# The order of the retention's normalization and of the weight splits, and of the small loads' waits, in a two-block transformer kernel

## The chip, the core and the metric

The kernel runs as one program on one core of a Trainium2 chip. The metric is the device time of one execution in microseconds (us). Five engines work side by side, each through its own list of instructions in order, held back only by semaphores: TensorE (PE: matmuls, its weight loads shown as PEld), VectorE (DVE), ScalarE (ACT), GpSimd (POOL) and SyncE (SP), which issues most DMAs. ScalarE issues some small DMAs between its own instructions.

## The reference

Two transformer blocks one behind the other on x of 256 positions and 2048 features, float32. The part that matters here is the first block's token mixer, cut to what is computed:

```python
proj = h @ w_in                                   # q, k, v, g_ret, u, gate_r, gate_s
q, k = rope(q), rope(k) * 128 ** -0.5             # 8 heads, q and k 128 wide, v 256
scores = (q @ k^T) * decay                        # causal, one decay rate a head
ret = head_group_norm(scores @ v)                 # per position and head: mean, variance over 256
y_ret = (silu(g_ret) * ret) @ w_ret_out
y_ssm = gelu(s5_ssm(u))                           # 64 groups, 64 complex states each, a scan over positions
y_s5 = glu(y_ssm @ w_s5_glu)
merged = sigmoid(gate_r) * y_ret + sigmoid(gate_s) * y_s5
x = x + gt_m * rmsnorm(merged @ w_out) * gain     # then a SwiGLU block, then the second block
```

h is rmsnorm(x) scaled and shifted by a modulation that is itself a product of a vector c with the 2048 x 12288 matrix w_ada. A wide gated feed-forward follows, and a second block with another mixer and feed-forward.

## The kernel before

**Weights.** Every weight matrix comes in tiles of 1 MB (128 x 2048 words), through a ring of four slots. SyncE waits until TensorE is through with a slot (`slot_free`) and issues the next tile. ScalarE copies the tile to its rounded high part (`split_hi`, L1006, out ring_hi), VectorE subtracts that from the tile to get the low part (`split_lo`, L1490, out ring_lo). The low part overwrites the raw tile. TensorE then multiplies, in this stage with three matmuls a piece (L636 to L638). Step m of a stage splits the tile of step m + 2: that is `ahead(p, g, m)`, the same call on ScalarE and VectorE.

**Start (0 to about 150 us).** SyncE issues c, x, then in turns a pair of rows of w_ada (two slots of the ring) and a piece of the value weights. ScalarE issues the small loads (`start`): bias, gains, then six more counted by the semaphore `start_in`. ScalarE squares x tile by tile, TensorE adds the squares up with a matrix of ones (`add_squares(0)`, L685), ScalarE takes the root, VectorE multiplies each row pair by c (`row_pair`, L1512) and makes one scaled tile of h of it. TensorE multiplies the values of all heads as the tiles come (L730).

**Stage "heads".** Two heads an iteration g, four iterations, eight steps m of one weight tile each: q, k and the gate's two halves for either head. The first iteration is written out, the other three are a hardware loop. The products of head n come in steps with r = m mod 4. The work of the head before lies between them:

- r = 0: VectorE takes the turned output of head n - 1 times its gate (`ret_out`, L1723) and masks the scores of head n (`ret_masked`, L1750); TensorE multiplies these with the values (`ret_values`, L753 to L755) behind its product.
- r = 1: VectorE takes mean and variance of that product (`ret_stats`, L1734 to L1738); ScalarE takes the root (`ret_std`, L1167).
- r = 2: VectorE inverts it and makes the shift (`ret_scale`, L1743, L1744); ScalarE applies both (`ret_normed`, L1172) and prepares the decay of the next head (`ret_decay`, L1179, L1180); VectorE rotates q and k (`rotate`, L1763 to L1768), which empties the accumulator.
- r = 3: TensorE multiplies q and k (`ret_scores`, L748) and transposes the normalized output (`ret_back`, L761); ScalarE evacuates the gate (L1186).

**The state-space part** runs through the same steps of "heads" and the next stage, "ret". For each of 32 state tiles TensorE multiplies the input (L713); VectorE turns the result back and scans it (`s5_turned_back`, L1696 to L1703, at odd m); POOL turns it on (`turned_on`, L2215 to L2218) and scales the output matrix (`c_scaled`, L2225, L2227); TensorE multiplies these (L703). The sine and cosine tables of two state tiles are made by POOL's `angles` (L2199), ScalarE's `waves` (L1108 to L1110, at m = 6 and m = 1) and `cosines` (L1117, L1118), and POOL's `sines` (L2205). `s5_turned_back` at m = 1 waits for the tables that `sines(0)` finishes. At m = 2 VectorE and ScalarE alternate in a gelu (`s5_gelu`, L1711 to L1718).

**Stage "ret"** multiplies the merge gates and the retention's output weights, four iterations. Its first steps carry what is left of the last head; the last two pieces of its fifth product wait for that head's finished output (L1729). Nothing in the order is made by a scheduler: all of it is written out by hand.

## Time and profile before

| | |
|---|---|
| time, median of 3 runs | 3425.26 us (3423.00 to 3428.01) |
| the profiled execution's own time | 3423.0 us |
| its span | 3421.2 us |
| TensorE busy | 3321.9 us (97%) |
| VectorE busy | 2358.4 us (69%) |
| ScalarE busy | 1470.7 us (43%) |
| POOL busy | 421.8 us (12%) |
| DMA, mean over the span | 206 GB/s; 380 in the first fortieth |
| chain that ended last | TensorE 80%, VectorE 10%, issue 3%, ScalarE 2%, DMA 2% |

The busy shares are means over stages with different limits. "Idle before" in a timeline's row, in square brackets, is the time in which the engine stood still ahead of that instruction, with the one that released it. A row that merges several instructions runs from the first start to the last end.

### The profile page before, as it was taken

The numbers are of one execution on the slowest core, as the hardware profiler recorded it, in microseconds if no ns is written. First come the engines' busy times: TensorE is split into PE (matmuls) and PEld (weight loads), VectorE is DVE, ScalarE is ACT, GpSimd is POOL, SyncE is SP. The second block draws the span as 40 slices with busy tenths as digits, with TensorE's granted clock in tenths as the row PEclk, the third lists the DMA queues.
The fourth block names the chain that finished last, engine by engine and source line by source line (L and its number), as shares of the span: only waits on it lengthen the run. The fifth ranks groups of instructions, "written<-read, shape, count | busy, mean of one in ns | idle before, by whom it ended". The sixth has DMA issues, their size and how long they took to land.

```text
span 3421.2 us, 52033 instructions
## 1 busy us (share of the span) xinstructions
PE 3321.9 (97%) x20368; PEld 2944.1 (86%) x20368; DVE 2358.4 (69%) x2479; ACT 1470.7 (43%) x1504; POOL 421.8 (12%) x309
## 2 busy tenths in 40 slices
PE   7999999999989999999989999999999999999998
PEld 3598898899978888888868888888888888888887
DVE  6699889977676666656676567657677766666554
ACT  2256565444444444433354443443434444444332
POOL 1046567700200000000000000000002100000000
PEclk9999999999999999999999999999999999999999
DMA  9884445577735555567724444555555555554554
GB/s 380 346 315 164 166 179 208 223 295 301 270 135 185 194 185 192 188 244 264 261 99 168 164 161 181 188 184 190 185 194 191 185 192 188 187 193 182 192 190 147
DMA packets 126274, 706.34 MB, mean 206 GB/s; under 512 B 14160, under 2 KB 41424, under 8 KB 47840
## 3 DMA queue, kind: packets, MB, share of 16 engines
q1 hardware_dynamic: 115808, 695.96, 55.0%
q10 hardware_dynamic: 10368, 9.02, 0.8%
q8 instruction: 68, 1.11, 0.1%
q14 instruction: 30, 0.25, 0.0%
HBM read 702.83 MB, written 2.10 MB: 206 GB/s over the span
## 4 chain that ended last, share of the span: by engine, by line
PE 80%; DVE 10%; issue 3%; ACT 2%; DMA 2%; SPq 2%; POOL 1%; DVEq 0%; ACTq 0%; POOLq 0%
PE acc L639 44%; PE acc L640 24%; PE acc L636 3%; PE acc L638 3%; PE acc L637 3%; DVE ring_lo L1490 2%; SPq L543 1%; DVE ring_raw L1512 1%; DMA ring_raw<-w_ada 1%; ACT ring_hi L1006 1%; DVE s_w L1696 0%; PE p_norm L685 0%; DVE s_v L1697 0%; DMA ring_raw<-w_ret 0%; DVE aside_y L1512 0%
## 5 line engine op out<-in xcount | busy, mean ns | idle before, releaser
L1490 DVE TENSOR_TENSOR ring_lo<-ring_raw,ring_hi 128x2048 fp32r<-128x2048 f32 (+2 forms) x560 | 1277.2, 2282 | 564.2 <-ACT ring_hi L1006 563.0
L639 PE MATMUL acc<-h_split,ring_hi 128*128 128x512 f32 x4736 | 1655.7, 392 | 9.2 <-DVE h_split L1552 4.5
L640 PE MATMUL acc<-h_split,ring_lo 128*128 128x256 f32 x4736 | 1337.6, 282 | 0.0
L1006 ACT ACTIVATE ring_hi<-ring_raw 128x2048 fp32r<-128x2048 f32 (+2 forms) x560 | 1040.6, 1862 | 411.6 <-DMA ring_raw<-w_down 150.9
L639 PEld LDWEIGHTS acc<-h_split,ring_hi 128*128 128x128 f32 x4736 | 891.8, 188 | 197.3 <-issue 9.7
L640 PEld LDWEIGHTS acc<-h_split,ring_lo 128*128 128x128 f32 x4736 | 897.8, 190 | 0.4
L639 PE MATMUL acc<-ffn_split,ring_hi 128*128 128x512 f32 x1408 | 488.2, 390 | 0.0
L640 PE MATMUL acc<-ffn_split,ring_lo 128*128 128x256 f32 x1408 | 397.1, 282 | 0.0
L2157 POOL TENSOR_TENSOR sq_sum<-sq_sum,tile 128x256 f32<-128x256 f32 x60 | 77.1, 1286 | 2565.4 <-ACT tile L1032 2565.4
L636 PE MATMUL acc<-h_split,ring_hi 128*128 128x256 f32 x1152 | 328.1, 285 | 5.5 <-DVE ring_lo L1490 3.1
L637 PE MATMUL acc<-h_split,ring_hi 128*128 128x256 f32 x1152 | 321.6, 279 | 0.0
L638 PE MATMUL acc<-h_split,ring_lo 128*128 128x256 f32 x1152 | 321.4, 279 | 0.0
L639 PEld LDWEIGHTS acc<-ffn_split,ring_hi 128*128 128x128 f32 x1408 | 264.4, 188 | 55.4
L640 PEld LDWEIGHTS acc<-ffn_split,ring_lo 128*128 128x128 f32 x1408 | 266.1, 189 | 0.0
L636 PEld LDWEIGHTS acc<-h_split,ring_hi 128*128 128x128 f32 x1152 | 216.6, 188 | 7.6 <-issue 2.9
L637 PEld LDWEIGHTS acc<-h_split,ring_hi 128*128 128x128 f32 x1152 | 216.6, 188 | 0.9 <-issue 0.2
L638 PEld LDWEIGHTS acc<-h_split,ring_lo 128*128 128x128 f32 x1152 | 216.5, 188 | 0.0
L1323 ACT ACTIVATE ffn_split<-ffn_a 128x256 f32 (+1 forms) x88 | 36.9, 420 | 358.0 <-DVE ffn_a L1914 358.0
L1505 DVE TENSOR_REDUCE ffn_b<-acc 128x256 f32<-128x512 f32 x88 | 60.9, 692 | 140.3 <-PE acc L640 140.2
L1032 ACT ACTIVATE tile<-x_res 128x256 f32 (+1 forms) x80 | 33.2, 418 | 150.1 <-DVE x_res L2138 84.1
L1321 ACT ACTIVATE ffn_t<-ffn_a 128x256 f32<-128x256 f32 x88 | 36.9, 419 | 130.6 <-DVE ffn_a L1910 119.4
L1512 DVE CUSTOM_DVE_ANT_0 ring_raw<-ring_raw,c_act 128x2048 f32<-128x2048 f32 x32 | 72.8, 2294 | 28.3 <-DMA ring_raw<-w_ada 28.3
(384 smaller groups left out, 3994.9 us busy)
## 6 DMA issues: line engine op xcount, KB each, us to landing
ring_raw<-w_ff SPq DMA_DIRECT2D x88, 1024.0 KB, 4.8
ring_raw<-w_down SPq DMA_DIRECT2D x64, 1024.0 KB, 4.8
ring_raw<-w_ffb SPq DMA_DIRECT2D x56, 1024.0 KB, 4.8
ring_raw<-w_mix SPq DMA_DIRECT2D x48, 1024.0 KB, 4.8
ring_raw<-w_ada SPq DMA_DIRECT2D x32, 1024.0 KB, 11.0
ring_raw<-w_heads SPq DMA_DIRECT2D x32, 1024.0 KB, 4.9
ring_raw<-w_ret SPq DMA_DIRECT2D x32, 1024.0 KB, 5.3
ring_raw<-w_glu SPq DMA_DIRECT2D x32, 1024.0 KB, 4.8
```

What stands on the lines that cost most here:

```text
L636: mm(dst[:, 0:T], hi[s][:, t, :], moving[:, k, 0:T], start=start, stop=False)
L637: mm(dst[:, 0:T], hi[s][:, t, :], moving[:, k, T:], start=False, stop=False)
L638: return mm(dst[:, 0:T], lo[s][:, t, :], moving[:, k, 0:T], start=False, stop=stop)
L639: mm(dst[:], hi[s][:, t, :], moving[:, k, :], start=start, stop=False, skip_group_check=True)
L640: return mm(dst[:, T:], lo[s][:, t, :], moving[:, k, 0:T], start=False, stop=stop, skip_group_check=True)
L1006: run(hi[s][:, 0:n, :], raw[s][:, 0:n, :], COPY).then_inc(hi_done, 1)
L1321: run(t[i % 2][:], a[i % 2][:], ACT.Tanh, scale=0.5).then_inc(f_tanh, 1)
L1323: run(dst[:, 4 * g + (first + i), 0:T], a[i % 2][:], COPY, scale=0.5).then_inc(f_hi, 1)
L1490: tt(lo[s][:, 0:n, :], raw[s][:, 0:n, :], hi[s][:, 0:n, :], SUB).then_inc(lo_done, 1)
L1505: v.tensor_reduce(dst, acc[o % 2][:].rearrange("p (c t) -> p t c", c=2), AX_X, ADD).then_inc(sum_done, 1)
L1512: v.tensor_tensor_reduce(weights, weights, c_act[:], 1.0, 0.0, MUL, ADD, ada_sum[:, i:i + 1]).then_inc(done, 1)
L2157: tt(sq_sum[:], sq_sum[:], tile[b][:], ALU.add).then_inc(sq_used, 1)
```

## The change

No instruction is added or taken away. There are four parts.

**Waits for the small loads.** The load of `gains` moves into the group counted by `start_in`, behind s5_a, so the group has seven. TensorE waits for all seven ahead of the first sum of squares, VectorE ahead of the first row pair (where it waited for bias and gains), ScalarE where it waited for six. Ahead of the heads stage TensorE waits for ScalarE's first exponential (`s5_trig`), no more for the loads.

**ScalarE.** `ret_normed` is called ahead of `ahead` at r = 2, in "heads" and in the opening of "ret".

**VectorE.** At r = 1 `ret_stats` is called behind `ahead` and behind `s5_turned_back`; in the opening of "ret" behind `ahead`, and there ahead of `s5_turned_back`. At r = 2 `rotate` is called behind `ahead`.

**POOL.** The fourth `c_scaled` and `turned_on` of a group come ahead of `sines(0)` and `angles`.

```diff
@@ TensorE
             pe.wait_ge(ones_set, 2)
+            pe.wait_ge(start_in, 16 * 7)
             add_squares(0)
...
             pe.wait_ge(v_evac, 8)
-            pe.wait_ge(start_in, 16 * 6)
+            pe.wait_ge(s5_trig, 1)
@@ ScalarE, start()
                 act.dma_start(b_ada[:], dram["b_ada_c"]).then_inc(bias_in, 16)
-                act.dma_start(gains[:], dram["gains"]).then_inc(bias_in, 16)
-                for dst, name in ((s5_a, "s5_a"), (ident, "identity"), (rope, "rope"),
+                for dst, name in ((s5_a, "s5_a"), (gains, "gains"), (ident, "identity"), (rope, "rope"),
                                   (lag, "lag"), (log_g, "log_g"), (s5_d, "s5_d")):
@@ ScalarE, heads
+                    if r == 2 and some(n):
+                        ret_normed(n)
                     ahead(p, g, m)
                     s5_steps("heads", g, m, early=True)
...
                     elif r == 2:
-                        if some(n):
-                            ret_normed(n)
                         ret_decay(n)
@@ ScalarE, ret
+                    if opening(g) and m == 2:
+                        ret_normed(HEADS)
                     ahead(p, g, m)
...
-                        elif m == 2:
-                            ret_normed(HEADS)
@@ VectorE, start
-            dve.wait_ge(bias_in, 16 * 2)
+            dve.wait_ge(bias_in, 16)
+            dve.wait_ge(start_in, 16 * 7)
@@ VectorE, heads
-                    if r == 0 and some(n):
+                    if r == 2 and some(n):
+                        ret_scale(n)
+                    elif r == 0 and some(n):
                         if some(n - 1):
                             ret_out(n - 1)
                         ret_masked(n)
-                    elif r == 1 and some(n):
-                        ret_stats(n)
-                    elif r == 2:
-                        if some(n):
-                            ret_scale(n)
-                        rotate(p, g, m - 1, n)
                     ahead(p, g, m)
                     if r == 0 and some(n):
                         ret_gated(n)
                         if some(n - 1):
                             ret_done(n - 1, n - 2)
+                    elif r == 2:
+                        rotate(p, g, m - 1, n)
                     s5_turned_back("heads", g, m)
+                    if r == 1 and some(n):
+                        ret_stats(n)
                     s5_gelu("heads", g, m)
@@ VectorE, ret (opening only)
-                        elif m == 1:
-                            ret_stats(HEADS)
...
                     ahead(p, g, m)
                     if opening(g):
                         if m == 0:
                             ret_gated(HEADS)
                             ret_done(HEADS - 1, HEADS - 2)
+                        elif m == 1:
+                            ret_stats(HEADS)
@@ POOL, s5_group
                 turned_on(2, 4 * g + 2)
+                c_scaled(3, 4 * g + 3, 2 * g + 2)
+                turned_on(3, 4 * g + 3)
                 if not end:
                     sines(0, 2 * g + 2)
                     angles(2 * g + 3)
-                c_scaled(3, 4 * g + 3, 2 * g + 2)
-                turned_on(3, 4 * g + 3)
```

What stands in a row on ScalarE at m = 1 and m = 2 of the loop of "heads", before (ring_hi is the high part of a weight tile, o_t the normalized output, s_ph and s_sin the waves, ret_scale the semaphore of VectorE's L1744; ISA and REGISTER_ALU rows only set addresses and waits):

```order
L1167 ACTIVATE gn_mean<-gn_mean,eps 128x2 [waits ret_var]
L1107 REGISTER_ALU
L1108 ACT_TABLE_LOAD
L1108 ACTIVATE s_sin<-s_ph 128x512 [waits s5_angle]
L1109 ACTIVATE s_ph<-s_ph 128x512
L191 REGISTER_ALU
L1110 ACTIVATE s_ph<-s_ph,eps 128x512 [waits act_own]
L1005 ISA
L1006 ACTIVATE ring_hi<-ring_raw 128x2048 [waits raw_in0]
L1172 ACTIVATE o_t<-p_o,gn_shift,gn_mean 128x256 [waits ret_scale]
L1172 ACTIVATE o_t<-p_o,gn_shift,gn_mean 128x256
```

and with the change (line numbers from there on are one higher):

```order
L1167 ACTIVATE gn_mean<-gn_mean,eps 128x2 [waits ret_var]
L1107 REGISTER_ALU
L1108 ACT_TABLE_LOAD
L1108 ACTIVATE s_sin<-s_ph 128x512 [waits s5_angle]
L1109 ACTIVATE s_ph<-s_ph 128x512
L191 REGISTER_ALU
L1110 ACTIVATE s_ph<-s_ph,eps 128x512 [waits act_own]
L1172 ACTIVATE o_t<-p_o,gn_shift,gn_mean 128x256 [waits ret_scale]
L1172 ACTIVATE o_t<-p_o,gn_shift,gn_mean 128x256
L1006 ISA
L1007 ACTIVATE ring_hi<-ring_raw 128x2048 [waits raw_in0]
```

The high part's copy stood ahead of the normalization and now stands behind it; the root and the waves are where they were.

What stands in a row on VectorE at m = 5 and the beginning of its turn-back, before (ring_lo is the low part of a weight tile, s_w and s_v the state-space part):

```order
L1734 BN_STATS gn_stats<-p_o 128x6 [waits ret_summed,dve_own]
L1735 BN_STATS gn_stats<-p_o 128x6
L191 REGISTER_ALU
L1736 MEMSET gn_shift 128x2 [waits dve_own]
L1737 BN_AGGR gn_mean<-gn_stats 128x2
L1738 BN_AGGR gn_mean<-gn_stats 128x2
L1489 REGISTER_ALU
L1490 TENSOR_TENSOR ring_lo<-ring_raw,ring_hi 128x2048 [waits hi_done]
L1689 REGISTER_ALU
L1690 REGISTER_ALU [waits z_done]
L1696 TENSOR_TENSOR s_w<-p_z,s_tab 128x512 [waits scan_done,s5_sine,s5_cos]
L1697 TENSOR_TENSOR s_v<-p_z,s_tab 128x512
```

and with the change, from the same statistics on, into m = 6 (qk_rot is the rotation):

```order
L1735 BN_STATS gn_stats<-p_o 128x6 [waits ret_summed]
L1736 BN_STATS gn_stats<-p_o 128x6
L191 REGISTER_ALU
L1737 MEMSET gn_shift 128x2 [waits dve_own]
L1738 BN_AGGR gn_mean<-gn_stats 128x2
L1739 BN_AGGR gn_mean<-gn_stats 128x2
L1744 RECIPROCAL gn_mean<-gn_mean 128x2 [waits ret_std]
L191 REGISTER_ALU
L1745 SCALAR_TENSOR_TENSOR gn_shift<-gn_mean 128x2 [waits dve_own]
L1489 REGISTER_ALU
L1490 TENSOR_TENSOR ring_lo<-ring_raw,ring_hi 128x2048 [waits hi_done]
L1762 REGISTER_ALU [waits ret_done]
```

The statistics stood ahead of the low part's copy and of the whole turn-back, and now come directly ahead of the inverse and the shift; the next copy now stands ahead of the rotation.

What stands in a row on POOL at the end of its first group, before (s_tab is the sine table, s_ph the angles):

```order
L2218 TENSOR_TENSOR s_x<-s_x,s_w 128x256
L2205 TENSOR_TENSOR s_tab<-s_sin,s_ph 128x512 [waits s5_waves]
L2199 TENSOR_TENSOR s_ph<-s_turn 128x512 [waits s5_sine]
L2225 TENSOR_TENSOR s_prod<-s_c_sb,s_f 128x128 [waits s5_c_in1]
L2227 TENSOR_TENSOR s_c_sb<-s_prod 128x2x32 [waits pool_own]
L2215 TENSOR_TENSOR s_x<-s_w,s_tab 128x512 [waits y_part,s5_scanned]
L2216 TENSOR_TENSOR s_w<-s_w,s_tab 128x512
L2217 TENSOR_TENSOR s_x<-s_w,s_x 128x256 [waits pool_own]
L2218 TENSOR_TENSOR s_x<-s_x,s_w 128x256
```

and with the change:

```order
L2218 TENSOR_TENSOR s_x<-s_x,s_w 128x256
L2225 TENSOR_TENSOR s_prod<-s_c_sb,s_f 128x128 [waits s5_c_in1]
L2227 TENSOR_TENSOR s_c_sb<-s_prod 128x2x32 [waits pool_own]
L2215 TENSOR_TENSOR s_x<-s_w,s_tab 128x512 [waits y_part,s5_scanned]
L2216 TENSOR_TENSOR s_w<-s_w,s_tab 128x512
L2217 TENSOR_TENSOR s_x<-s_w,s_x 128x256 [waits pool_own]
L2218 TENSOR_TENSOR s_x<-s_x,s_w 128x256
L2205 TENSOR_TENSOR s_tab<-s_sin,s_ph 128x512 [waits s5_waves]
L2199 TENSOR_TENSOR s_ph<-s_turn 128x512 [waits s5_sine]
```

The sine table and the angles stood ahead of the fourth state tile's steps and now stand behind them.

## Rows read from the trace of the kernel before

**Rows 1.** windows: us, busy us (instructions) by engine, clock, DMA share, GB/s

```profile
205.00:455.00 250.00, 231.90 (x1779) 224.15 (x1778) 228.03 (x272) 150.24 (x170) 149.27 (x111) 0.99 0.50 183
```

**Rows 2.** waits of TensorE, 205 to 455: who, for whom, us, times, longest

```profile
PE p_o L753 <- DVE scores L1750: 16.0, 8, 3.6
```

**Rows 3.** timeline, VectorE, odd half: start, us, line, operation [idle before <-releaser]

```profile
302.81 0.43 DVE L1734 BATCH_NORM_STATS2 gn_stats<-p_o 128x6 f32<-128x256 f32 x1
...
303.78 2.26 DVE L1490 TENSOR_TENSOR ring_lo<-ring_raw,ring_hi 128x2048 fp32r<-128x2048 f32 x1
...
309.53 1.27 DVE L1744 SCALAR_TENSOR_TENSOR gn_shift<-gn_mean 128x2 f32<-128x2 f32 x1
...
312.84 1.25 DVE L1768 TENSOR_TENSOR qk_rot<-qk_rot,qk_sin 128x512 f32<-128x512 f32 x1
...
319.05 3.02 DVE L1490 TENSOR_TENSOR ring_lo<-ring_raw,ring_hi 128x2048 fp32r<-128x2048 f32 x1 [2.75 <-ACT ring_hi L1006]
...
325.97 0.55 DVE L1750 SCALAR_TENSOR_TENSOR scores<-p_score,scores 128x384 f32<-128x384 f32 x1
```

**Rows 4.** timeline, ScalarE, odd half

```profile
303.89 0.30 ACT L1167 ACTIVATE gn_mean<-gn_mean,eps 128x2 f32<-128x2 f32 x1 [5.22 <-DVE gn_mean L1738]
304.10 1.90 ACT L1006 ACTIVATE ring_hi<-ring_raw 128x2048 fp32r<-128x2048 f32 x1
310.84 1.02 ACT L1172 ACTIVATE o_t<-p_o,gn_shift,gn_mean 128x256 f32<-128x256 f32 x2 [4.84 <-DVE gn_shift L1744]
311.88 1.28 ACT L1179 ACT_TABLE_LOAD   x1
...
314.00 1.28 ACT L1108 ACT_TABLE_LOAD   x1
...
317.11 1.91 ACT L1006 ACTIVATE ring_hi<-ring_raw 128x2048 fp32r<-128x2048 f32 x1
```

**Rows 5.** timeline, VectorE, even half

```profile
330.57 1.23 DVE L1729 SCALAR_TENSOR_TENSOR ret_split<-qk_sin,ret_split 128x512 f32 x1
...
340.65 0.94 DVE L1768 TENSOR_TENSOR qk_rot<-qk_rot,qk_sin 128x512 f32<-128x512 f32 x1
...
350.38 2.29 DVE L1490 TENSOR_TENSOR ring_lo<-ring_raw,ring_hi 128x2048 fp32r<-128x2048 f32 x1 [1.23 <-ACT ring_hi L1006]
...
356.80 0.55 DVE L1750 SCALAR_TENSOR_TENSOR scores<-p_score,scores 128x384 f32<-128x384 f32 x1
```

**Rows 6.** timelines of VectorE and POOL: a copy, and POOL's work beside such

```profile
225.19 2.82 DVE L1490 TENSOR_TENSOR ring_lo<-ring_raw,ring_hi 128x2048 fp32r<-128x2048 f32 x1
...
225.81 3.36 POOL L2205 TENSOR_TENSOR s_tab<-s_sin,s_ph 128x512 f32<-128x512 f32 x1
...
331.21 1.19 POOL L2218 TENSOR_TENSOR s_x<-s_x,s_w 128x256 f32<-128x256 f32 x1
```

**Rows 7.** timelines of ScalarE and VectorE, opening of the ret stage

```profile
458.42 0.30 ACT L1167 ACTIVATE gn_mean<-gn_mean,eps 128x2 f32<-128x2 f32 x1 [0.85 <-DVE gn_mean L1738]
...
466.44 0.99 ACT L1172 ACTIVATE o_t<-p_o,gn_shift,gn_mean 128x256 f32<-128x256 f32 x2
...
479.11 0.69 DVE L1729 SCALAR_TENSOR_TENSOR ret_split<-qk_sin,ret_split 128x512 fp32r<-128x512 f32 x1 [0.70 <-ACT ret_split L1163]
...
518.09 0.69 DVE L1696 TENSOR_TENSOR s_w<-p_z,s_tab 128x512 f32<-128x512 f32 x1 [0.64 <-POOL s_x L2218]
```

**Rows 8.** the start: a DMA issue (xcount, KB, us to landing), then timelines

```profile
s_d_sb<-s_d ACTq DMA_DIRECT2D x1, 4.0 KB, 14.7
...
4.74 0.52 ACTq L1080 DMA_DIRECT2D s_d_sb<-s_d  x1
...
11.02 10.81 PE L685 MATMUL p_norm<-tile,ones 128*128 128x256 f32 x32 [11.02 <-ACT tile L1032]
...
28.38 3.96 SPq L527 DMA_DIRECT2D ring_raw<-w_ada  x4
...
38.17 2.29 DVE L1512 CUSTOM_DVE_ANT_0 ring_raw<-ring_raw,c_act 128x2048 f32<-128x2048 f32 x1 [5.20 <-DMA ring_raw<-w_ada]
```

More of the change, by code:

```diff
@@ L1066, in s5_waves_begin @@
             def s5_waves_begin():
-                act.wait_ge(start_in, 16 * 6)
+                act.wait_ge(start_in, 16 * 7)
                 run(s5_t[:, 0, :], s5_a[:, 2, :], ACT.Exp).then_inc(s5_trig, 1)
@@ L1809, in _ @@
                 for m in range(8):
-                    if opening(g):
-                        if m == 0:
-                            ret_out(HEADS - 1)
-                            ret_masked(HEADS)
-                        elif m == 1:
-                            ret_stats(HEADS)
-                        elif m == 2:
-                            ret_scale(HEADS)
+                    if opening(g) and m == 2:
+                        ret_scale(HEADS)
+                    elif opening(g) and m == 0:
+                        ret_out(HEADS - 1)
+                        ret_masked(HEADS)
                     ahead(p, g, m)
```

## The prediction

> **What bounds the kernel now.** I read first the windows of the whole span by engine, then who waits for whom, then the timeline of each engine through one iteration of the stage where TensorE waits. In the heads stage (about 205 to 455 us) TensorE is busy 231.90 of 250 us, VectorE 228.03 [rows 1]: two engines are near their limit at once, so what is put late on VectorE has little room. The wait list of TensorE there has one large entry: eight waits of 16.0 us together for the masked scores of L1750 [rows 2]. So the stage runs at the pace of the chain that ends in L1750, and nothing behind it has room either (TensorE is busy 97% of the whole span, in the small table above); a microsecond added to that chain is a microsecond of the kernel.
>
> One iteration of the stage is two heads. I call the steps from one L1750 to the next the odd half (m = 4 to 7, then L1750 at m = 0) and the even half (m = 0 to 3, then L1750 at m = 4). The timelines show both: L1750 ends at 326.52 and at 357.35 [rows 3, 5]. What the reader is to see in them: VectorE idles before its weight copies for ScalarE (2.75 us before the copy at 319.05 in the odd half, 1.23 us before that at 350.38 in the even half), and ScalarE in turn idles for VectorE (5.22 us before the square root, 4.84 us before `ret_normed`, L1172) [rows 3 to 5]. ScalarE gets its weight split (L1006, 304.10) done inside that second idle time. The two engines hand work back and forth, and each hand-over's place in the order is the whole question.
>
> **The change in the heads stage.** It adds no instruction. Statistics (L1734 and on) come behind the low-part copy and the turn-back of the state-space part; `ret_normed` comes ahead of ScalarE's weight split; on VectorE the rotation comes behind the copy that waits for that split. Read together: the split of tile m + 2 now stands behind `ret_normed`, which stands behind `ret_scale`, which stands behind the statistics. What was a free filler has become a link in the chain.
>
> Odd half, from 302.81, where the statistics began [rows 3, 4]. Copy 2.26 -> 305.07. Turn-back with the reciprocal: from the end of the copy (306.04) to the start of L1744 (309.53) 3.49 -> 308.56. Statistics 302.81 to 303.78, 0.97 -> 309.53. Square root 0.30 -> 309.83. L1744 took 1.27 beside POOL; I take that -> 311.10. `ret_normed` 1.02 -> 312.1. Weight split 1.90 -> 314.0, against 306.00 before. VectorE waits for it, then copies 2.26 -> 316.3, then rotates (310.80 to 314.09, 3.29) -> 319.6, against 314.09. ScalarE goes on with the decay (311.88 to 314.00, 2.12) -> 316.1, the waves (to 317.11, 3.11) -> 319.2, the next split 1.91 -> 321.1, against 319.02. VectorE's copy 2.26 -> 323.4, and from there to the end of L1750 it is 4.45 (322.07 to 326.52) -> 327.9. That is 1.4 us late. The rise is small because the 2.75 us of idle time takes most of it in. Bounds: 0.1 if L1744 (two values per row) costs next to nothing once POOL lets go of it, 2.2 if the last copy keeps its 3.02. In the first iteration VectorE also multiplies modulation rows at every second step, and has no such idle time to give: 1.4 + 2.75 = 4.1 (the lower bound stays 0.1). Four odd halves: 4.1 + 3 x 1.4 = 8.3.
>
> Even half, from 331.80, the end of L1729 [rows 5]. Copy 2.26, turn-back 3.49, statistics 0.97, square root 0.30 -> 338.8. Here ScalarE has the waves next (m = 1), which used to run while VectorE turned back: 3.11 -> 341.9. Only then `ret_normed` 1.02 -> 342.9 and the split 1.90 -> 344.8. VectorE, ready since about 339, waits; copy 2.26 -> 347.1; rotation 3.29 -> 350.4, against 341.59. From the rotation's end to the next copy it was 8.79 (341.59 to 350.38), of which the copy now done was 2.82, as long as that at 225.19 [rows 6]: 5.97 -> 356.4. From there to the end of L1750 it is 6.97 -> 363.3, against 357.35: 6.0 late. Nothing gives this back, since TensorE is the one that waits at the end of it. Bounds 5.4 (part of the two short waits on ScalarE inside the gelu chain goes) and 6.6 (the copy takes 2.8). Three even halves: 18.0.
>
> ScalarE's switches of function table are in these sums at their measured length: the load at 311.88 takes 1.28 and the function follows at once [rows 4]. The Trainium skill (ScalarE: Activation LUTs, What ACT_TABLE_LOAD costs) gives 2.66 us for each switch, 1.38 of it a drain. By that rule the wave step alone would make each even half 1.4 dearer, 4 us in all; the row shows no drain, so the row stands.
>
> **The opening of the next stage.** The last head is handled the same way at m = 1 and 2 of the ret stage. Its square root was at 458.42 and its `ret_normed` at 466.44 [rows 7]. The root moves behind a copy and the turn-back (2.26 + 3.3), to 464.0. Then 0.30, a table load 1.28, a gate's evacuation (short like the root, taken at 0.4), the waves 3.11 -> 469.1, so `ret_normed` is 2.7 late, and the split and the copy behind it (0.99 + 1.90 + 2.26) end at 474.3, some 5.4 late. The last two tiles of the fifth product wait for this head's finished output (L1729, 479.11, and it idled 0.70 there [rows 7]). I take 4.7, one short wait being given back; bounds 2.7 and 5.4.
>
> **The change on POOL.** The fourth `turned_on` now comes ahead of `sines(0)` and `angles`. Before, these filled a wait. Now `sines(0)` starts when L2218 ends (331.21 + 1.19 = 332.40) [rows 6], just when VectorE's moved copy is running, and the turn-back at m = 1 waits for it. The nearest row is L2205 at 225.81: started 0.62 behind a copy of VectorE (225.19) it took 3.36 [rows 6]. So 332.4 + 3.4 = 335.8, against 334.1 when VectorE arrives: 1.7. If nothing held it, it would take some 1.3 as its companions do, 333.7, and cost nothing; so 0 to 1.7, and I take 1.7, by that row. It stands before every even half and the ret opening: 4 x 1.7 = 6.8. In the ret stage the turn-back at 518.09 already waits for L2218 [rows 7], so one L2205 of 1.3 comes on top once: 8.1 in all, bounds 0 and 8.1.
>
> The Trainium skill (SBUF — State Buffer, Who interferes with whom) says that a VectorE instruction with two SBUF inputs and a GpSimd instruction that reads SBUF exclude each other for the whole instruction, whoever came first. By that rule `sines(0)` behind the copy costs what I took; the trace agrees at 225.81, where L2205 ends 1.16 behind the end of the copy (228.01).
>
> **The change at the start.** TensorE's sum of squares and VectorE's first row pair now wait for seven small loads. The last, s_d_sb, is issued at 4.7 and lands 14.7 later, 19.4 [rows 8]. TensorE began at 11.02 and took 10.81 [rows 8], so the norm comes 8.4 later. Behind it on TensorE stand the value products, on VectorE all row pairs. But the third pair's rows landed only at 38.17, after 5.20 us of idle time of VectorE [rows 8]: the transfers set the pace there, and its delay is taken in. The engines must not run dry meanwhile. Slots are freed at most 8.4 later, so their refills are issued at most 8.4 later, and rows issued at 28.38 land at 38.17 [rows 8], a backlog of 9.8. I cost it at nothing; if that cover is gone it is the full 8.4. Below nothing it can't go, since nothing is earlier. The new wait of the heads stage (for the exponential in place of the loads) is satisfied long before.
>
> **Sum.** 8.3 + 18.0 + 4.7 + 8.1 = 39.1. The profiled execution took 3423.0 (span 3421.2 and 1.8 around it), so 3462.1; the median of the three runs is 2.3 above the profiled one, so I state 3464. Its own range: low end 4 x 0.1 + 3 x 5.4 + 2.7 + 0 = 19.3, 3444; high end 4.1 + 3 x 2.2 + 3 x 6.6 + 5.4 + 8.1 = 44.0, 3469.
>
> **Rivals.** All are on the same base of 3425.
> - POOL's edit is free because `sines(0)` slips in between VectorE's instructions. Terms without 8.1: 31.0, 3456. For it: L2218 at 331.21, beside VectorE's work, took only 1.19 [rows 6]. Against: 225.81.
> - The even half costs no more than the odd one, as TensorE and VectorE regroup so that the waves lie under other work: 8.3 + 3 x 1.4 + 2.7 = 15.2, 3441. Against: ScalarE runs in order, and the waves stand between the root and `ret_normed`.
> - The start is not covered: a gap in the DMA stream is never made up, 8.4 more, 3472. For it: 8.4 is not far below the backlog of 9.8, and a gap is there for good once it is. Against: the 5.20 us of idle time, which shows that the data, not the slots, were late.
> - Faster: the point is the wait of TensorE for L1750. If ScalarE had the split done by the time VectorE asks for it, the earlier copy and earlier transposes would remove those waits, at most 16.0, 3409. It decides at one place: whether the split of tile m + 2 ends before `ret_scale` does. In the working above it ends 2.9 (314.0 against 311.1, odd) and some 5.8 (344.8 against about 339, even) behind.
> - The edits do nothing measurable: the reordered instructions have slack everywhere. The 16.0 us of waits speak against.
>
> **Numbers.** Forecast 0.65, free POOL edit 0.15, cheap even half 0.07, uncovered start 0.07, faster 0.04, nothing 0.02. A difference within 0.2% (7 us) is what a measurement of this kernel can't tell from none. Slower 0.94, same 0.02, faster 0.04. The range 3444 to 3476 takes in both ends of the sum and the start partly or wholly uncovered; it leaves out the cheap even half, the fast case and the null.
>
> **What would show it.** In the profile after: ScalarE's weight split behind `ret_normed` in both halves; VectorE idle some 3 and some 6 us for "ring_hi" before the copies of m = 6 and m = 2; TensorE's waits for the masked scores well above 16.0, and new ones of some 3 us for the rotated q and k ahead of the scores product; an even half, from one masked-scores instruction to the next, of some 38.5 us where it was 30.8 (326.52 to 357.35); the turn-back at m = 1 waiting for POOL; the sum of squares beginning at 19.4 and the third row pair still near 38. I am wrong if the even half stays near 31, or if the delay of the start is still there at 150 us.

## The result, and the profile after it

The changed kernel takes 3453.52 us, the median of four runs (3450.71 to 3458.48), against 3426.29 for the kernel before in the same series (3423.00 to 3428.01). The ratio is 1.0083, 95% interval 1.0064 to 1.0100: slower by some 28 us, within 22 to 34. The profiled execution took 3455.24, its span 3453.5.

The waits of TensorE in the heads stage, columns as in [rows 2]:

```profile
PE p_score L749 <- DVE qk_rot L1769: 16.8, 6, 3.6
PE p_o L754 <- DVE scores L1751: 16.0, 7, 4.8
```

The wait for the masked scores is no larger than in [rows 2]. A second one of the same size has come: for the rotated q and k. The stage as a whole, columns as in [rows 1], 276 us where there were 250:

```profile
206.00:482.00 276.00, 241.98 (x1781) 232.61 (x1780) 222.86 (x274) 150.04 (x170) 137.25 (x110) 0.95 0.46 164
```

VectorE is busy 222.86 us against 228.03 [rows 1]: it has not more to do, it stands still. (TensorE's 241.98 against 231.90 us are nearly the same instructions, 1781 and 1779, at a granted clock of 0.95 in place of 0.99; the last section says what that cost.) Where VectorE stands still, its timeline says. The odd half, against [rows 3]:

```profile
318.39 0.41 DVE L1735 BATCH_NORM_STATS2 gn_stats<-p_o 128x6 f32<-128x256 f32 x1
...
323.96 2.29 DVE L1490 TENSOR_TENSOR ring_lo<-ring_raw,ring_hi 128x2048 fp32r<-128x2048 f32 x1 [2.89 <-ACT ring_hi L1007]
...
331.10 2.29 DVE L1490 TENSOR_TENSOR ring_lo<-ring_raw,ring_hi 128x2048 fp32r<-128x2048 f32 x1 [2.11 <-ACT ring_hi L1007]
...
337.29 0.55 DVE L1751 SCALAR_TENSOR_TENSOR scores<-p_score,scores 128x384 f32<-128x384 f32 x1
```

The 2.75 us of [rows 3] have become 2.89 and 2.11. The half grows by only 1.5 us, because VectorE's instructions take 1.2 less in it (busy 27.46 us between 374.36 and 407.97, where it was 28.68 between 356.80 and 388.91): POOL runs beside fewer of them. The even half, against [rows 5] and [rows 6]:

```profile
343.05 2.82 DVE L1490 TENSOR_TENSOR ring_lo<-ring_raw,ring_hi 128x2048 fp32r<-128x2048 f32 x1
347.11 0.69 DVE L1697 TENSOR_TENSOR s_w<-p_z,s_tab 128x512 f32<-128x512 f32 x1 [1.24 <-POOL s_tab L2205]
...
358.21 2.29 DVE L1490 TENSOR_TENSOR ring_lo<-ring_raw,ring_hi 128x2048 fp32r<-128x2048 f32 x1 [4.54 <-ACT ring_hi L1007]
...
362.54 0.69 DVE L1769 TENSOR_TENSOR qk_rot<-qk_rot,qk_sin 128x512 f32<-128x512 f32 x1
...
364.11 0.29 DVE L1714 TENSOR_SCALAR s_g<-s_g 128x256 f32<-128x256 f32 x1 [0.48 <-ACT s_g L1148]
...
368.17 2.29 DVE L1490 TENSOR_TENSOR ring_lo<-ring_raw,ring_hi 128x2048 fp32r<-128x2048 f32 x1 [1.23 <-ACT ring_hi L1007]
...
374.36 0.55 DVE L1751 SCALAR_TENSOR_TENSOR scores<-p_score,scores 128x384 f32<-128x384 f32 x1
```

and ScalarE in it:

```profile
351.95 0.30 ACT L1167 ACTIVATE gn_mean<-gn_mean,eps 128x2 f32<-128x2 f32 x1 [9.71 <-DVE gn_mean L1739]
352.26 1.28 ACT L1108 ACT_TABLE_LOAD   x1
...
355.37 1.00 ACT L1172 ACTIVATE o_t<-p_o,gn_shift,gn_mean 128x256 f32<-128x256 f32 x2
356.27 1.91 ACT L1007 ACTIVATE ring_hi<-ring_raw 128x2048 fp32r<-128x2048 f32 x1
...
363.66 0.42 ACT L1148 ACTIVATE s_g<-s_y 128x256 f32<-128x256 f32 x1 [2.09 <-DVE s_y L1712]
```

The root of the same half in the kernel before:

```profile
332.80 0.30 ACT L1167 ACTIVATE gn_mean<-gn_mean,eps 128x2 f32<-128x2 f32 x1 [1.87 <-DVE gn_mean L1738]
```

From masked scores to masked scores it is 37.07 us (337.29 to 374.36) where it was 30.83 (325.97 to 356.80). Three pieces: up to ScalarE's root 14.66 (351.95) against 6.83 (332.80); from there to the copy that waits 1.23, 16.22 against 17.58 (350.38 in [rows 5]); and 6.19 against 6.42. The root is 7.8 us later, and 1.6 come back behind it. The root waits for the statistics, hence ScalarE's 9.71 us of idle time. VectorE's busy time in the half is the same as before (27.37 and 27.38 us): all of the 6.2 us is waiting.

The start of the program, against [rows 8]:

```profile
19.68 5.60 PE L685 MATMUL p_norm<-tile,ones 128*128 128x256 f32 x15 [19.68 <-DMA s_d_sb<-s_d]
```

```profile
38.55 2.29 DVE L1512 CUSTOM_DVE_ANT_0 ring_raw<-ring_raw,c_act 128x2048 f32<-128x2048 f32 x1
```

The sum of squares is 8.66 us late, the third row pair 0.38: the 5.20 us in which VectorE waited for the transfer [rows 8] are used up, and no more was needed. ScalarE's first weight split stands where it stood, at 147.06 (147.14 before), so nothing of the delay is left at 150 us.

### The profile page after: what moved, and what is told of

Its sections match the earlier page's. It is cut to its first block, busy times and chain, and to the rows that moved or that the text cites. A ratio compares the mean times of both kernels' runs of the same rounds, so it can differ in the third digit from the quotient of the medians.

```text
span 3453.5 us, 52031 instructions
## 1 busy us (share of the span) xinstructions
PE 3330.1 (96%) x20368; PEld 2951.9 (85%) x20368; DVE 2346.6 (68%) x2479; ACT 1468.3 (43%) x1504; POOL 412.9 (12%) x309
## 4 chain that ended last, share of the span: by engine, by line
PE 78%; DVE 8%; issue 4%; POOL 4%; ACT 3%; DMA 2%; SPq 1%; ACTq 0%; DVEq 0%; POOLq 0%
PE acc L639 44%; PE acc L640 23%; PE acc L636 3%; PE acc L637 3%; PE acc L638 3%; DVE ring_lo L1490 1%; ACT ring_hi L1007 1%; DVE ring_raw L1512 1%; POOL s_w L2216 1%; POOL s_x L2218 1%; PE p_norm L685 1%; POOL s_x L2215 1%; DMA ring_raw<-w_ada 1%; SPq L543 1%; POOL s_tab L2205 1%
## 5 line engine op out<-in xcount | busy, mean ns | idle before, releaser
L1490 DVE TENSOR_TENSOR ring_lo<-ring_raw,ring_hi 128x2048 fp32r<-128x2048 f32 (+2 forms) x560 | 1273.2, 2275 | 595.2 <-ACT ring_hi L1007 593.7
L637 PEld LDWEIGHTS acc<-h_split,ring_hi 128*128 128x128 f32 x1152 | 219.8, 191 | 0.9 <-issue 0.2
L639 PE MATMUL acc<-mixed_split,ring_hi 128*128 128x512 f32 x256 | 90.0, 394 | 0.0
```

The costliest lines, as they stand in the source:

```text
L637: mm(dst[:, 0:T], hi[s][:, t, :], moving[:, k, T:], start=False, stop=False)
L639: mm(dst[:], hi[s][:, t, :], moving[:, k, :], start=start, stop=False, skip_group_check=True)
L1490: tt(lo[s][:, 0:n, :], raw[s][:, 0:n, :], hi[s][:, 0:n, :], SUB).then_inc(lo_done, 1)
```

## The experiments

All were measured the same way. An iteration of the heads stage repeats to 0.1 or 0.2 us inside a run, so the table gives the distances between masked-scores instructions (us, read from each kernel's timeline of VectorE) beside the times. *Span of eight* is from the first to the eighth of them; where single ones differ (by 0.5 at most) the table gives their mean.

| kernel | first odd | odd | even | span of eight | median us | ratio (95%) |
|---|---|---|---|---|---|---|
| before | 30.9 | 32.1 | 30.7 | 219.3 | 3426.3 | |
| changed | 33.2 | 33.6 | 37.1 | 245.4 | 3453.5 | 1.0083 (1.0064-1.0100) |
| start_only | 30.9 | 32.1 | 30.7 | 219.2 | 3422.8 | 0.9996 (0.9986-1.0006) |
| act_only | 32.5 | 33.9 | 30.6 | 226.0 | 3430.7 | 1.0016 (1.0007-1.0026) |
| stats_only | 32.1 | 32.8 | 33.2 | 230.3 | 3435.9 | 1.0035 (1.0021-1.0049) |
| rotate_only | 30.9 | 32.1 | 30.8 | 219.5 | 3423.0 | 1.0000 (0.9990-1.0010) |
| pool_only | 30.2 | 31.5 | 31.7 | 219.8 | 3427.3 | 1.0004 (0.9995-1.0014) |
| after_no_pool | 34.2 | 34.3 | 35.6 | 244.1 | 3449.8 | 1.0072 (1.0055-1.0089) |
| after_no_rotate | 32.9 | 33.7 | 34.9 | 238.9 | 3447.8 | 1.0067 (1.0052-1.0083) |
| after_no_stats | 32.6 | 33.2 | 32.9 | 230.8 | 3440.5 | 1.0042 (1.0027-1.0058) |
| after_waves | 33.2 | 33.7 | 36.5 | 243.7 | 3451.8 | 1.0080 (1.0063-1.0096) |
| after_ret_waves | 33.2 | 33.7 | 37.1 | 245.6 | 3453.9 | 1.0093 (1.0076-1.0110) |
| masked_early | - | - | - | 216.6 | 3423.3 | 0.9995 (0.9986-1.0005) |
| masked_splits | - | - | - | 210.2 | 3415.0 | 0.9973 (0.9962-0.9985) |

The two last rows have their masked scores at m = 3 and 7, so their halves are others; an iteration is 62.8 and 60.1 us in them, 62.8 before, 70.7 with the change. The ratio of each experiment is to runs of the kernel before beside it (medians 3422.9 to 3425.4); the times of different rows are a little less comparable than the spans.

### The five parts, each alone

The diff of each is its part of the change as shown above. **start_only.** 

> The kernel before with the start's part of the change alone (gains counted with the small loads, all seven waited for ahead of the first sum of squares and the first row pair). Theory: the sum of squares begins near 19.5 in place of 11.0, and the transfers of the modulation's rows take the delay in; the first masked scores of the heads stage come at most 1.0 us later than the 232.25 of before, and the whole is within 2 us of before. Rival (a gap at the start is never made up): 8.4 us slower, first masked scores near 240.6.

The first masked scores are at 232.11, against 232.25. The start's part costs nothing. (In the changed kernel they are at 233.30, and about as late in act_only, 233.23, which leaves the start alone. Up to there the traces differ by 1 to 2 us whatever the edit; most of it comes at about 142 us, from TensorE's clock, as the last section shows.)

**act_only.** 

> The kernel before with ScalarE's part alone (the normalization ahead of the weight split). Theory (ScalarE is the pace-maker behind the normalization): decay, waves and the next split come one split (1.9 us) later, VectorE waits 4.65 in place of 2.75 before its copy in the odd half, and each of seven halves is 1.9 longer: 13 us slower. Rival (the edits cost only together, since the split is ahead of the statistics' chain as long as these are early): within 2 us of before.

Half right. In the odd half VectorE waits 4.53 as expected and the half is 1.8 longer. The even half is not longer at all: VectorE is the late one in the gelu there (in the kernel before ScalarE idles 1.71 us ahead of its L1148 at 344.75), so a split's delay on ScalarE is taken in (the 1.71 are 0.45 here, before L1148 at 349.49). 6.6 us in this stage, 7 in the median, where 13 were expected.

**stats_only.** 

> The kernel before with VectorE's late statistics alone (behind the copy and the turn-back). Theory: the split stands behind the root on ScalarE, so it is late even without the other edit; odd halves 0.9 longer, even halves 2.3 to 4.6 longer since the waves stand between the root and the split: 11 to 17 us slower, most of it in the even halves. Rival (the statistics have room, only the normalization ahead of the split makes the chain): within 2 us of before.

Odd 0.7 (first 1.2), even 2.5: the lower end of what was expected, 11.0 in this stage, 12 in the median. The rival is out. The theory holds for the odd half: VectorE waits 3.61 us for the split where it waited 2.75. In the even half the split is late, too (16.3 us behind the masked scores, 10.3 before), but the copy does not wait for it, as the rotation still stands ahead of it:

```profile
342.85 1.20 DVE L1744 SCALAR_TENSOR_TENSOR gn_shift<-gn_mean 128x2 f32<-128x2 f32 x1
...
347.67 3.14 DVE L1490 TENSOR_TENSOR ring_lo<-ring_raw,ring_hi 128x2048 fp32r<-128x2048 f32 x1
```

There 1.0 of the 2.4 us from 329.40 to 362.66 is waiting for ScalarE (0.36 for the root, 1.08 in place of 0.49 before the gelu's L1713), and 1.5 is VectorE's own instructions, which run beside other work of POOL (busy 28.85 us in place of 27.38; L1744 took 0.16 at 338.42 in the kernel before). The expectation had the right size there for the wrong reason.

**rotate_only.** 

> The kernel before with the rotation behind the low part's copy alone. Theory: VectorE does the same work in the other order, the scores product had stood in line behind TensorE's own product until 316.3 anyway; within 2 us of before. Rival (the scores product is what the masked scores wait for): 2.3 us later in each half, 16 us slower.

Free, as the theory had it: 0.2 us in the stage.

**pool_only.** 

> The kernel before with POOL's part alone (the fourth turn-on ahead of the sine table and the angles). Theory of the prediction: the turn-back at m = 1 waits for the sine table that runs beside the copy, 1.7 us before each even half, at most 8.1 in all. Reading of the changed kernel's trace: that wait is 1.24 there (347.11), so 1.2 in each of three even halves and 0.4 in the opening of ret, 3 to 5 us slower. Rival (the table slips in between): within 1 us.

In this stage only 0.5 us, but by two effects of opposite sign: even halves 1.0 longer, odd ones 0.6 shorter. Behind it, from the last masked scores to the weight split at 660 us, it is 3.6 more, so 4.1 in this trace. The medians show 2.0, and their interval (0.9995 to 1.0014) tells that neither from nothing nor from the 3 to 5 expected.

What the five add to the span of eight is -0.1, 6.6, 11.0, 0.2 and 0.5, 18.2 us in sum. Together they make 26.0. Nearly 8 us come only from the company. (All of these are for the heads stage alone.)

### One part taken back

**after_no_rotate.** 

> The changed kernel with the rotation back ahead of the low part's copy. Theory (the late split alone costs VectorE little as long as the rotation, 3.3 us of ready work, stands ahead of the copy that waits for it; behind the copy it holds the gelu up): the wait before the copy of m = 2 falls from 4.54 to about 1.3, the gelu begins 2 us sooner, ScalarE's 2.09 us of idle time before it go; the even half falls from 37.1 to 35.1, the odd half stays at 33.6 (there ScalarE's next split sets the time), 6 us faster than the changed kernel. Rival (the whole loss is in the statistics and ScalarE's order, the rotation is as free here as it was alone): both halves as in the changed kernel, within 2 us.

```diff
 VectorE, heads, r == 2
                         ret_scale(n)
+                    rotate(p, g, m - 1, n)      # and not behind ahead
```

As expected: 34.9 and 33.7, 5.7 us in the median. The same edit is worth 0.2 us alone and 6.5 in company (245.4 less 238.9). Its VectorE in the even half:

```profile
354.65 2.29 DVE L1490 TENSOR_TENSOR ring_lo<-ring_raw,ring_hi 128x2048 fp32r<-128x2048 f32 x1 [0.83 <-ACT ring_hi L1007]
...
358.35 0.30 DVE L1714 TENSOR_SCALAR s_g<-s_g 128x256 f32<-128x256 f32 x1 [1.02 <-ACT s_g L1148]
```

The copy waits 0.83 where it waited 4.54, since the rotation fills the time; and now the gelu waits for ScalarE and not the reverse.

**after_no_stats.** 

> The changed kernel with the statistics back ahead of the copy and the turn-back. Theory (ScalarE's root is the head of its chain to the split of m = 3, and it is 7.8 us late only because the statistics are): the root comes 6.8 us behind the masked scores again, the even half is 31.6 (30.8 and POOL's 1.0), the odd half 33.3 (the 1.8 of the normalization ahead of the split, less 0.6), some 16 us faster than the changed kernel, 3437. Rival (the normalization ahead of the split, with the rotation behind the copy, is the chain, and the statistics are only carried along): even half 35 or more, less than 6 us faster.

```diff
 VectorE, r == 1
+                        ret_stats(n)            # ahead of ahead, as before; the same in the opening of ret
```

The largest part: 14.6 us of the 26.0. The odd half is 33.2 as expected, the even one 32.9 and not 31.6. ScalarE and VectorE show why:

```profile
343.27 0.63 ACT L1108 ACTIVATE s_sin<-s_ph 128x512 f32<-128x512 f32 x1 [2.36 <-POOL s_ph L2199]
346.13 1.02 ACT L1172 ACTIVATE o_t<-p_o,gn_shift,gn_mean 128x256 f32<-128x256 f32 x2 [0.94 <-DVE gn_shift L1745]
...
348.98 2.51 DVE L1490 TENSOR_TENSOR ring_lo<-ring_raw,ring_hi 128x2048 fp32r<-128x2048 f32 x1 [2.89 <-ACT ring_hi L1007]
```

The root is back (6.8 us behind the masked scores), and the waves behind it wait 2.36 us for POOL's angles. That wait costs nothing here: it is over 0.94 us before the normalization gets VectorE's shift, and in pool_only it is as long (2.35). Up to the shift the two kernels run alike, 13.43 us from the masked scores. What is left is what the expectation forgot: with the normalization ahead of the split and the rotation behind the copy, VectorE has nothing to do until the split is there, 2.89 us. Of that, 1.7 come back, as its instructions down to the gelu take less time than in pool_only (the gelu's TENSOR_SCALAR 0.29 where it took 1.14), and the even half is 1.1 longer than pool_only's in all.

**after_no_pool.** 

> The changed kernel without POOL's part. Theory: the even half falls from 37.1 by the 1.24 us that the turn-back waited for POOL, to 35.9, and the whole is 3 to 5 us faster than the changed kernel. Rival (the wait is taken in by what comes behind it): even half still 37.1.

Even half 1.5 shorter, a little more than the 1.24; odd half 0.7 longer; 3.7 us in the median. Whence the odd half's part? VectorE's last copy of the odd half there:

```profile
330.67 3.02 DVE L1490 TENSOR_TENSOR ring_lo<-ring_raw,ring_hi 128x2048 fp32r<-128x2048 f32 x1 [2.12 <-ACT ring_hi L1007]
```

and POOL beside it:

```profile
330.48 1.06 POOL L2199 TENSOR_TENSOR s_ph<-s_turn 128x512 f32 x1 [0.28 <-POOL s_tab L2205]
```

It is the 3.02 of [rows 3]. With POOL's part the sine table and the angles have gone from here, and the copy takes 2.29 (331.10 above). They stand beside the even half's first copy in place of it:

```profile
343.68 3.34 POOL L2205 TENSOR_TENSOR s_tab<-s_sin,s_ph 128x512 f32<-128x512 f32 x1
```

3.34 where it takes 1.29 with nothing beside it (328.91 in after_no_pool), as [rows 6] had shown at 225.81. The collision was not made, it was moved, from a place where it cost 0.7 to one where it costs 1.5.

### Two tests of the mechanism

**after_waves.** 

> The changed kernel, but in the heads stage the waves of m = 1 stand behind the weight split of m = 2 on ScalarE, in place of ahead of the normalization. Theory (the waves between root and normalization are what makes the even half dear): normalization and split come 3.1 minus the 1.3 that the scaling takes anyway, some 1.9 us sooner; the even half falls from 37.1 towards 35.2, 5 to 6 us faster over three. Rival (the even half is dear because the gelu chain with its hand-overs follows behind, and the waves only change places): even half 37 or longer, since the waves now delay decay and cosines.

```diff
 ScalarE, heads: not at the end of m = 1 but
                     elif r == 2:
+                        if m == 2: waves(1, 2 * g + 1)
                         ret_decay(n)
```

0.6 to 0.7 us an even half, not 1.9: nearer to the rival. VectorE:

```profile
355.62 2.29 DVE L1492 TENSOR_TENSOR ring_lo<-ring_raw,ring_hi 128x2048 fp32r<-128x2048 f32 x1 [2.89 <-ACT ring_hi L1007]
...
362.54 0.29 DVE L1716 TENSOR_SCALAR s_g<-s_g 128x256 f32<-128x256 f32 x1 [1.45 <-ACT s_g L1148]
```

The split does come sooner (2.89 of wait in place of 4.54), but now the gelu waits 1.45 for ScalarE. From the late root to the end of the gelu ScalarE has the same work in any order. So the waves' place between root and normalization is not what makes the even half dear; that the root itself is late, and all of ScalarE's work stands behind it, is.

**after_ret_waves.** 

> The changed kernel, but in the ret stage ScalarE's waves of m = 1 stand behind the weight split of m = 2 (the heads stage is untouched). POOL's part of the change cost 2.8 us in this stage, where one of 1.3 was forecast. Theory (ScalarE's waves wait 3.62 us for POOL's angles, which now stand behind the fourth turn-on, and hold up the split and VectorE's copy behind them): the copy of m = 2 waits no more for the split (1.28 and 1.17 in the changed kernel), and up to 3 us of the ret stage are got back, 3451. Rival (it is VectorE's turn-back, which waits 2.03 us for the sine table itself, and moving ScalarE's waves changes nothing): within 1 us of the changed kernel at the end of the stage.

```diff
 ScalarE, ret: waves(1, ...) at m = 2 behind ahead, in place of m = 1
```

The copy's wait for the split is gone (1.28 before L1490 at 551.66), but the gelu behind it now waits 2.19 us for ScalarE where it waited 0.57, and the time is the same (3453.9). VectorE still has:

```profile
546.67 0.69 DVE L1700 TENSOR_TENSOR s_w<-p_z,s_tab 128x512 f32<-128x512 f32 x1 [2.04 <-POOL s_tab L2208]
```

The rival holds at this place. Compared split by split on ScalarE, after_no_pool is 26.9 us behind the kernel before at 489 us and 27.0 at 660, the changed kernel 28.2 and 31.1: POOL's part costs 2.8 us in between. This kernel, too, has 31.1 at 660. It entered the stage 1.3 us earlier (last masked scores at 477.41, not 478.67), lost that in the opening (the gelu waits 2.18), and is level with the changed kernel from there on. What makes up the 2.8 beside the wait of 2.04 was not taken apart.

### Is there more to gain?

**masked_early.** 

> The kernel before, with the masked scores (L1750) taken ahead of the copy at m = 3 and m = 7, one step earlier, where VectorE stood idle for ScalarE. Theory (the 16.0 us of TensorE's waits in the heads stage are VectorE's order, not its amount of work): these waits vanish, and 8 to 16 us of the kernel with them. Rival (VectorE is full, the wait moves to the copy that the next product needs): within 4 us of before.

```diff
 VectorE, heads
-                        ret_masked(n)           # r == 0
+                    elif r == 3:
+                        ret_masked(n + 1)       # ahead of ahead; the call in the opening of ret goes
```

The rival was right in size. The wait went over to TensorE's next product, not the one that the rival named: to L713, which waits until VectorE's turn-back has emptied p_z:

```profile
PE p_z L713 <- DVE s_v L1697: 12.6, 6, 2.9
```

The 16.0 us of [rows 2] were the place where TensorE met VectorE's pace, not a cost of that order.

**masked_splits.** 

> The kernel before with three moves in the heads stage: the masked scores ahead of the copy at m = 3 and 7; ScalarE's waves of m = 6 behind the split of m = 7; ScalarE's split of m = 3 ahead of the gelu of m = 2. Theory (with the masked scores early the iteration's 62.8 us are VectorE's 58.2 of work and 4.65 of waiting for ScalarE, of which 2.18 and 0.76 go): 59.9 an iteration, 10 us faster over three and a half, 3415. Rival (the period is held by something that these rows don't show, as with the masked scores alone): within 3 us of before.

```diff
 ScalarE, heads, on top of masked_early
+    waves(0, ...)   # at m = 7 behind ahead, in place of m = 6
+    ahead(p, g, 3)  # at m = 2 ahead of the gelu, in place of m = 3
```

An iteration of 60.1 (59.9 expected), 3415.0 us: 0.9973 (0.9962 to 0.9985), the fastest kernel here. VectorE's two waits for splits are gone; in an iteration only the gelu's three hand-overs are left, 1.7 us together. Whether ScalarE's two moves would do it without the early masked scores was not run. TensorE's waits:

```profile
PE p_z L713 <- DVE s_v L1703: 7.1, 4, 2.9
PE acc L636 <- DVE ring_lo L1496: 2.6, 3, 0.9
```

## Why the prediction was right, and where its sizes were off

The direction and the chain were right, and the time lies in the range, 10.5 us under the forecast. From the first to the eighth masked scores it is 26.0 us more, in the opening of ret 1.1, by POOL behind it 2.8: 29.9 where the sum had 39.1, and some 28 by the ratio.

**Odd halves:** 2.3 + 3 x 1.5 = 6.8, forecast 8.3. The 1.4 of the loop was 1.5. The bound of 2.2, "if the last copy keeps its 3.02", is what after_no_pool shows (34.3 less 32.1); what frees the copy is POOL's edit, which the step had not said. The first half cost 2.3, not 4.1 (3.3 without POOL's edit): VectorE, which idled nowhere in it, now waits 2.89 and 0.36 us, and its instructions take 1.0 less.

**Even halves:** without POOL's part 4.9 each (35.6 less 30.7), forecast 6.0. The mis-sized piece is the one from the rotation's end to the next copy: 4.94 us (363.23, the end of L1769, to 368.17) where 5.97 was put, 1.03 too much. It was read off a gelu that ran beside POOL's work. Its slowest instruction in the kernel before:

```profile
345.21 1.12 DVE L1713 TENSOR_SCALAR s_g<-s_g 128x256 f32<-128x256 f32 x1 [0.49 <-ACT s_g L1148]
```

In the changed kernel it takes 0.29 (364.11); POOL is through by then (its L2199 ends at 358.17). And the reason given, the waves between root and `ret_normed`, is only a small part of it: after_waves.

**Opening of ret:** from the last masked scores (451.58 and 478.67) to the first product of the next weights (482.30 and 510.49) it is 1.1 more; the forecast was 4.7, and its bounds of 2.7 and 5.4 did not hold it. Here the step itself was wrong. It put the root "behind a copy and the turn-back", but in this stage the statistics come ahead of the turn-back. ScalarE:

```profile
488.27 0.30 ACT L1167 ACTIVATE gn_mean<-gn_mean,eps 128x2 f32<-128x2 f32 x1 [3.62 <-DVE gn_mean L1739]
...
493.39 1.00 ACT L1172 ACTIVATE o_t<-p_o,gn_shift,gn_mean 128x256 f32<-128x256 f32 x2
```

The root is 9.60 behind the masked scores, 6.84 before; `ret_normed` is at 14.72, 14.86 before [rows 7]: not late at all. By the forecast's own steps behind it, a root that is 2.8 late and not 5.6 makes the copy of m = 2 end 2.6 late, not 5.4, and that is what the traces show (19.87 behind the masked scores, 17.28 before); 1.4 of it come back in the gelu.

**POOL:** in the even halves 4.6 (19.3 with it, 14.7 without; forecast 5.1), in ret 2.8 (forecast 3.0). In the even halves the size was right. In ret its agreement is luck: 1.7 of the 3.0 were for the opening, where the turn-back waits only 0.39 (488.63) and after_no_pool is no faster, and the 1.3 behind it came out as 2.8. Not foreseen were the 3.2 that it gives back in the odd halves (10.0 without, 6.8 with it); so the edit costs 4.1 in all, half of the 8.1. That ScalarE's waves, too, wait for what was put late was not foreseen either.

**Start:** nothing, as forecast, but with the cover used up to the last: the third pair is 0.38 late. The rival of 8.4 is out.

**The signs:** the two waits for ring_hi (2.89 and 4.54; some 3 and 6 were named), the turn-back's wait for POOL (1.24) and those for the rotated q and k came. The even half was to be 38.5 and is 37.1. The wait for the masked scores did not rise; the likely reason is that the scores product stands ahead in TensorE's line and takes a part of the same delay, but no run separates the two.

**Rivals:** the cheap even half and the faster case are out by the halves. The free POOL edit, 3456, is nearest in time, but for another reason: the collision costs what was said, and gives back elsewhere. And what the faster case counted on, up to 16.0 us from TensorE's waits, was not there to be had: masked_early.

## What to carry to other kernels

Where two engines hand work back and forth, ask of each moved step what stands behind it on both: a late head of the other engine's line (here the root) delays all that follows, and the two orders behind it that were tried mend little (1.7 us with ScalarE's waves moved, 6.5 with the rotation, of 26.0). Price edits together: ready work kept ahead of a waiting instruction is worth nothing until something makes that instruction wait, and then it fills the wait (0.2 us alone, 6.5 in company). When a wait on the critical engine is large, first see whether its releaser is idle at all; taking that wait away gave nothing here, taking away the releaser's idle time as well gave 9 us.

## What the runs showed of the hardware that was not expected

A collision between POOL and VectorE is a price on either, by who came first: L2205 takes 3.34 beside a copy that began 0.63 ahead of it, 1.29 alone; the copy takes 3.02 behind an L2199 that began 0.19 ahead of it, 2.29 alone. That is what the Trainium skill (SBUF — State Buffer, Who interferes with whom) states of a VectorE instruction with two SBUF inputs and a GpSimd instruction that reads SBUF. The traces agree.

TensorE's granted clock fell behind waits. Stretches of 4 us of the changed kernel, columns as in [rows 1]:

```profile
368.00:372.00 4.00, 3.83 (x33) 3.62 (x32) 3.80 (x4) 2.43 (x3) 1.92 (x2) 1.00 0.06 21
372.00:376.00 4.00, 0.94 (x2) 0.83 (x3) 3.86 (x7) 1.46 (x3) 2.06 (x2) 0.77 0.72 254
376.00:380.00 4.00, 4.00 (x11) 3.13 (x10) 4.00 (x3) 1.49 (x1) 3.92 (x3) 0.50 0.12 41
```

Behind a stretch in which TensorE was busy 0.94 of 4 us it ran at 0.50, the level of 1.2 GHz, and its four matmuls of L713 took 1.78 us where the same took 1.03 at 340.25. It cost nothing in this stage: the even half from 337.29 has a mean clock of 0.95 and takes 37.07 us, the one from 407.97 has 1.00 and takes 37.09, and VectorE's list of waits in the stage does not name TensorE.

Whether the clock falls behind a wait is not the same in every execution. In the kernel before, and in the changed one:

```profile
141.09 1.99 PE L730 MATMUL acc<-wv_b,normed 128*128 128x512 f32 x4 [2.03 <-ACT normed L1093]
142.91 1.02 PE L730 MATMUL p_turn<-wv_b,normed 128*128 128x512 f32 x2
```

```profile
141.02 2.80 PE L731 MATMUL acc<-wv_b,normed 128*128 128x512 f32 x4 [1.94 <-ACT normed L1093]
143.62 1.91 PE L731 MATMUL p_turn<-wv_b,normed 128*128 128x512 f32 x2
```

Between 138 and 146 us the granted clock is 1.00 in the first and 0.79 in the second, and what stands behind comes 1.6 us later (ScalarE's third weight split at 155.63 and 157.25). It is not the edit: act_only and rotate_only run the instructions of the kernel before up to there, and have 0.79 and 157.41, and 1.00 and 155.62.
